# Gates and branch projections of two layers: from weights loaded and 256 token columns moving to tokens loaded and 512 weight columns moving

## What is computed

```python
h = rms_norm(x, norm1_g)
z = h @ w_in                      # the last 4 * 1024 columns of z are zg
...
ys = jnp.stack([ya, yb, yc, yd], axis=2)          # four branches, each 256 x 512
branches = jnp.einsum('bsnc,ncd->bsnd', ys, w_branch)   # four products of 512 x 1024
gates = jax.nn.sigmoid(zg.reshape(B, S, N_BRANCH_2, D_MODEL))
mix = jnp.sum(gates * branches, axis=2)
x = x + mix @ w_out
```

## Time and profile before

| | |
|---|---|
| median of 3 runs | 2144.68 us (2143.9 to 2147.41) |
| the profiled execution, its own time | 2145.49 us |
| its span, first to last instruction | 2144.2 us |
| TensorE (PE) busy | 2113.1 us, 99% |
| TensorE weight loads (PEld) busy | 1958.1 us, 91% |
| VectorE (DVE), ScalarE (ACT), GpSimd (POOL) busy | 65%, 58%, 46% |
| share of TensorE in the chain that ended last | 88% |
| mean granted TensorE clock | 0.998 |

### The profile page before, as it was taken

One profiled execution on the slowest core, in us unless ns is written; L12 is line 12 of the kernel. 1 busy time (PEld: TensorE's weight loads), 2 busy tenths in 40 slices (PEclk: granted clock), 3 DMA queues, 4 the chain that ended last, 5 costly groups with the idle time before them and its releaser, 6 DMA issues.

```text
span 2144.2 us, 37243 instructions
## 1 busy us (share of the span) xinstructions
PE 2113.1 (99%) x14292; PEld 1958.1 (91%) x14292; DVE 1395.7 (65%) x2706; ACT 1247.4 (58%) x2272; POOL 977.1 (46%) x791
## 2 busy tenths in 40 slices
PE   7999999999999999999999999999999999999999
PEld 7999989999999998888889899998888999998887
DVE  4467655998676756666667765557764864757874
ACT  5669454546777865455445465746555465756553
POOL 4776557999667650000004785660001876661000
PEclk9999999999999999999999999999999999999999
DMA  6444565655444456666665554555565645455565
GB/s 231 149 138 129 172 197 173 196 178 180 145 140 147 141 168 204 195 192 192 195 195 196 186 157 139 155 180 167 187 205 158 189 146 168 141 165 177 187 194 160
DMA packets 103952, 370.59 MB, mean 173 GB/s; under 512 B 11480, under 2 KB 12896, under 8 KB 103264
## 3 DMA queue, kind: packets, MB, share of 16 engines
q1 hardware_dynamic: 103776, 368.21, 54.8%
HBM read 366.05 MB, written 2.11 MB: 172 GB/s over the span
## 4 chain that ended last, share of the span: by engine, by line
PE 88%; DVE 6%; ACT 2%; POOL 1%; issue 1%; DMA 1%; SPq 0%; DVEq 0%; ACTq 0%; POOLq 0%
PE stream_bank L568 14%; PE stream_bank L570 14%; PE stream_bank L569 14%; PE side_bank L568 9%; PE side_bank L570 9%; PE side_bank L569 9%; PE side_bank L577 4%; PE stream_bank L577 4%; PE side_bank L574 2%; PE stream_bank L574 2%; PE side_bank L918 1%; PE side_bank L917 1%; POOL unit_lo L2606 1%; ACT unit_hi L1181 1%; PE side_bank L746 1%
## 5 line engine op out<-in xcount | busy, mean ns | idle before, releaser
L2606 POOL TENSOR_TENSOR unit_lo<-raw,unit_hi 128x512 fp32r<-128x512 f32 (+1 forms) x724 | 938.5, 1324 | 943.6 <-ACT unit_hi L1181 941.6
L1181 ACT ACTIVATE unit_hi<-raw 128x1024 fp32r<-128x1024 f32 (+1 forms) x678 | 708.9, 1046 | 199.5 <-PE side_bank L570 66.0
L1777 DVE TENSOR_TENSOR unit_lo<-raw,unit_hi 128x1024 fp32r<-128x1024 f32 (+1 forms) x316 | 390.3, 1236 | 227.9 <-ACT unit_hi L1181 225.9
L568 PE MATMUL stream_bank<-hT,unit_hi 128*128 128x256 f32 x1360 | 398.9, 293 | 1.8 <-POOL unit_lo L2606 1.8
L570 PE MATMUL stream_bank<-hT,unit_lo 128*128 128x256 f32 x1360 | 384.6, 283 | 0.0
L569 PE MATMUL stream_bank<-hT,unit_hi 128*128 128x256 f32 x1360 | 384.5, 283 | 0.0
L568 PE MATMUL stream_bank<-h2T,unit_hi 128*128 128x256 f32 x1024 | 293.3, 286 | 0.0
L570 PE MATMUL stream_bank<-h2T,unit_lo 128*128 128x256 f32 x1024 | 289.8, 283 | 0.0
L569 PE MATMUL stream_bank<-h2T,unit_hi 128*128 128x256 f32 x1024 | 289.6, 283 | 0.0
L568 PEld LDWEIGHTS stream_bank<-hT,unit_hi 128*128 128x128 f32 x1360 | 259.9, 191 | 3.6 <-POOL unit_lo L2606 2.0
L569 PEld LDWEIGHTS stream_bank<-hT,unit_hi 128*128 128x128 f32 x1360 | 260.0, 191 | 1.6
(11 more groups left out here) (392 smaller groups left out, 4303.9 us busy)
## 6 DMA issues: line engine op xcount, KB each, us to landing
raw<-in_peer_u_dram SPq DMA_DIRECT2D x128, 512.0 KB, 3.5
raw<-in_peer_v_dram SPq DMA_DIRECT2D x128, 512.0 KB, 4.1
raw<-in_gate_dram SPq DMA_DIRECT2D x64, 512.0 KB, 3.5
raw<-in_gt_dram SPq DMA_DIRECT2D x44, 512.0 KB, 3.5
raw<-in_up_dram SPq DMA_DIRECT2D x44, 512.0 KB, 3.5
raw<-in_ffn_out_dram SPq DMA_DIRECT2D x44, 512.0 KB, 3.5
raw<-in_branch_dram SPq DMA_DIRECT2D x32, 512.0 KB, 3.5
raw<-in_w_gate_dram SPq DMA_DIRECT2D x24, 512.0 KB, 3.5
```

Source lines behind the costliest of these rows:

```text
L568: mm(out, l.hi, r.hi, start=start, stop=False)
L1181: activation(k.unit_hi[n % SPLIT_SLOTS][:, 0:w], k.raw[n % RAW_SLOTS][:, 0:w], ACT.Copy).then_inc(k.sem("unit_hi"), 1)
L1777: V.tensor_tensor(k.unit_lo[s][:, 0:w], k.raw[n % RAW_SLOTS][:, 0:w], k.unit_hi[s][:, 0:w], ALU.subtract).then_inc(unit_lo, 1)
L2606: last = G.tensor_tensor(k.unit_lo[s][:, cols], k.raw[n % RAW_SLOTS][:, cols], k.unit_hi[s][:, cols], ALU.subtract)
```

## The change

1. The weight layouts of `gate` and `branch` become `tm_units(..., 2, 512)`. The number of units (32 + 16 in each layer) and their size stay.
2. A new `block_unit` multiplies them: 12 matmuls of 512 columns in place of 24 of 256. A block is 4 units of `gate` or 2 of a branch. It takes two of the three rotating banks, one for each token tile t; in each unit t = 0 comes first, so that the bank of t = 0 is finished half a unit before that of t = 1.
3. ScalarE evicts a whole block with two tanhs of 128 x 512 in the block's last round. In the other three rounds it does only `hi(n+3)` and its side steps.
4. VectorE sums a block in its last round (`add_branch`): for each of two banks a 128 x 512 product, and for branches 2 to 4 an addition.
5. The merged rows now have tokens on the partitions, and `w_out` needs features there: `turn_merged` turns them with 16 transposes of 128 x 128 in each layer, 8 behind the third unit of the last branch and 8 behind the first unit of `w_out`. ScalarE (`merged_hi`) and VectorE (`merged_lo`) split the turned banks.

The core of the diff:

```diff
+    def block_unit(key, block, units, u, lhs, banks):
+        i = block * units + u
+        n = U[key, i]
+        w = unit(n)
+        for t in range(TILES):
+            if u == 0:
+                banks.append(take(rotation[turn[0] % len(rotation)], (key, "block", block, t)))
+                turn[0] += 1
+            for c in range(2):
+                last = mm3(banks[t][:, :], lhs.at(lambda x: x[:, 2 * u + c, t * P:(t + 1) * P]),
+                           w.at(lambda x: x[:, c * 512:(c + 1) * 512]), u == 0 and c == 0, u == units - 1 and c == 1)
...
+    def turn_merged(label, x, half, ready):
+        for k2 in (2 * half, 2 * half + 1):
+            bank = take(SIDE + 2 + k2 % 2, (label, k2))
+            for t in range(TILES):
+                pe.wait_ge(*ready[2 * half + t])
+            for j in range(2):
+                c = 2 * k2 + j
+                for t in range(TILES):
+                    last = nc.tensor.transpose(bank[:, j * TOKENS + t * P:j * TOKENS + (t + 1) * P],
+                                               x[:, t, c * P:(c + 1) * P], k.ident)
+            last.then_inc(k.sem("merged_turned"), 1)
...
             for u in range(4):
                 tm_unit(key, half * 4 + u, lhs, 2 * u, 2, 512, banks, u == 0, u == 3, ready if half == 0 else None)
+                if half == 0 and u == 0 and behind_first is not None:
+                    behind_first()
...
# PE main()
-            for i in range(32):
-                fm_unit(name("gate"), i, k.hT2, KD)
-                yield
+            for block in range(8):
+                banks = []
+                for u in range(4):
+                    block_unit(name("gate"), block, 4, u, k.hT2, banks)
+                    yield
...
+                for half in range(2):
+                    banks = []
+                    for u in range(2):
+                        block_unit(name("branch"), 2 * n + half, 2, u, part, banks)
+                        if n == BRANCH_ORDER[-1] and half and u == 0:
+                            turn_merged(name("merged"), merged, 0, summed())
+                        yield
...
# ACT main()
-                evict(name("gate"), i, k.gates2[:, i, :], ACT.Tanh, scale=0.5)
+                advance(name("gate"), i)
+                if i % 4 == 3:
+                    for t in range(TILES):
+                        label = (name("gate"), "block", i // 4, t)
+                        act.wait_ge(*k.mm_done[label])
+                        activation(k.gates2[:, t, i // 4 * 512:(i // 4 + 1) * 512], k.bank[k.bank_of[label]][:, :], ACT.Tanh,
+                                   scale=0.5).then_inc(k.free[k.bank_of[label]], 1)
...
# DVE main(), and its add_branch
+                for i in range(KD // 2):
+                    advance(name("branch"), n * KD // 2 + i)
+                    if i % 2:
+                        add_branch(place, n, i // 2)
+                    if place == BRANCHES2 - 1 and i == 3:
+                        merged_lo(0)
+                    yield
...
+                dve.wait_ge(*k.mm_done[label])
+                if place == 0:
+                    V.scalar_tensor_tensor(gate, gate, 1.0, bank, ALU.add, ALU.mult).then_inc(k.free[b], 1)
+                    dve.wait_ge(*k.over[label])
+                else:
+                    own.then(V.scalar_tensor_tensor(bank, gate, 1.0, bank, ALU.add, ALU.mult))
+                    V.tensor_tensor(total, total, bank, ALU.add).then_inc(k.free[b], 1)
+                    dve.wait_ge(*k.over[label])
...
+        def merged_lo(half):
+            for k2 in (2 * half, 2 * half + 1):
+                b = SIDE + 2 + k2 % 2
+                dve.wait_ge(k.sem("mix_hi"), KD // 2 * l + k2 + 1)
+                V.scalar_tensor_tensor(k.hT2.lo[:, 2 * k2:2 * k2 + 2, :], k.bank[b][:, :].rearrange("p (a t) -> p a t", a=2),
+                                       0.5, k.hT2.hi[:, 2 * k2:2 * k2 + 2, :], ALU.mult, ALU.subtract).then_inc(k.free[b], 1)
```

More of the change, by code:

```diff
@@ L671, in close_banks @@
         at.unit = U[key, units - 1] + 1
+    def block_unit(key, block, units, u, lhs, banks):
[9 more added lines that the diff above has]
+                           w.at(lambda x: x[:, c * 512:(c + 1) * 512]), u == 0 and c == 0, u == units - 1 and c == 1)
+            if t == 0 and u == units - 1:
+                last.then_inc(tm_mm, 1)
+                tm_count[0] += 1
+                k.mm_done[key, "block", block, 0] = (tm_mm, tm_count[0])
+        last.then_inc(unit_mm, 1)
+        k.mm_done[key, "block", block, 1] = (unit_mm, n + 1)
+        at.unit = n + 1
+    def turn_merged(label, x, half, ready):
[9 more added lines that the diff above has]
+            last.then_inc(k.sem("merged_turned"), 1)
     def keep_warm(name):
@@ L1086, in swa @@
                 head(s, [(k.sem("swa_scaled"), 5 * l + 2 + s.column), k.over[name("sv"), 1]]) for s in heads])
+        merged = k.gates2[:, :, BRANCH_ORDER[0] * D:(BRANCH_ORDER[0] + 1) * D]
+        last_branch = lambda half, t: (name("branch"), "block", 2 * BRANCH_ORDER[-1] + half, t)
+        summed = lambda: {2 * h + t: k.over[last_branch(h, t)] for h in range(2) for t in range(TILES)
+                          if last_branch(h, t) in k.over}
         def main():
@@ L1698, in main @@
                     advance(name("branch"), n * KD // 2 + i)
[L1699 to L1702, removed]
+                    if n == BRANCH_ORDER[-1] and i == 3:
+                        merged_hi(0)
                     yield
@@ L1716, in sides, with merged_hi @@
             yield from at.finished(name("branch3"), swa())
+        def merged_hi(half):
+            for k2 in (2 * half, 2 * half + 1):
+                act.wait_ge(k.sem("merged_turned"), KD // 2 * l + k2 + 1)
+                split_hi(k.hT2.hi[:, 2 * k2:2 * k2 + 2, :],
+                         k.bank[SIDE + 2 + k2 % 2][:, :].rearrange("p (a t) -> p a t", a=2), "mix_hi", 0.5)
         at.run(main(), [bias_tables() if l == 0 else iter(()), own_channels(), sides()])
@@ L1720, in layer @@
             advance(name("w_out"), u)
+            if u == 0:
+                merged_hi(1)
         halves = [[((t, h), k.over[name("w_out"), h, t]) for t in range(TILES)] for h in range(2)]
@@ L2515, in main @@
                     yield
-                if place == 0:
[L2517 to L2536, removed]
@@ new lines, in main, with add_branch @@
+                for i in range(KD // 2):
[5 more added lines that the diff above has]
+                    yield
+        def add_branch(place, n, half):
+            for t in range(TILES):
+                label = (name("branch"), "block", 2 * n + half, t)
+                b = k.bank_of[label]
+                bank = k.bank[b][:, :]
+                gate = k.gates2[:, t, n * D + half * 512:n * D + (half + 1) * 512]
+                first = BRANCH_ORDER[0] * D + half * 512
+                total = k.gates2[:, t, first:first + 512]
+                if place == 0:
+                    dve.wait_ge(*k.over[name("gate"), "block", 2 * n + half, t])
+                dve.wait_ge(*k.mm_done[label])
[6 more added lines that the diff above has]
+                    dve.wait_ge(*k.over[label])
@@ L2552, in layer @@
         turned = norm_lo(name("n2"), name("norm2"), k.sumT)
-        add_out(name("w_out"), k.X, turned)
+        add_out(name("w_out"), k.X, turned, lambda: merged_lo(1))
         advance(name("w_out"), 7)
@@ L2935, in lay_out @@
         d[f"sq.{l}"], d[f"sk.{l}"], d[f"sv.{l}"] = fm_units(swa_q_columns(cut(7))), fm_units(cut(8)), tm_units(cut(9), 8, 128)
-        d[f"gate.{l}"] = fm_units(cut(10))
+        d[f"gate.{l}"] = tm_units(cut(10), 2, 512)
         b = wb[l].copy()
         b[3] = b[3].reshape(SWA_HEADS, SWA_DIM, D)[SWA_ORDER].reshape(MIX, D)
-        d[f"branch.{l}"] = np.concatenate([fm_unit_pairs(b[i]) for i in range(BRANCHES2)])
+        d[f"branch.{l}"] = np.concatenate([tm_units(b[i], 2, 512) for i in range(BRANCHES2)])
         d[f"w_out.{l}"] = tm_units(n["w_out_2"][l], 2, 512)
```

13 lines of the change are left out of this document (6 added, 7 removed).

## The result

The changed kernel takes 2147.11 us (median of 20 runs, 2145.34 to 2149.84), the kernel before, beside it, 2142.66 us (median of 20, 2139.11 to 2147.41). The ratio is 1.0019 with a 95% interval of 1.0013 to 1.0025. By the ratio that is +4.1 us (by the two medians +4.4) where +4.0 was forecast: a real loss, but one of only 0.2%.

The account below looks back on a forecast made before the run. TensorE, busy for 99% of the span, was taken as the bound. The terms -15.4 + 2.5 + 3.7 + 5.2 + 1.3 + 6.7 = +4.0 us made 2148.7 us from 2144.7, range 2139.5 to 2155.

Parts of the forecast that it names:

- The matmuls and their restarts: Gates and branches: wide matmuls save 15.4 us, 13.3 ns a merge; restarts behind side steps cost +2.5 us.
- The transposes: Four groups of eight for the merged rows, hidden by nothing: 0.92 us a group, +3.7 us.
- The turn ahead of `w_out`: TensorE waits for VectorE's `merged_lo` behind the last half's sum, until T + 2.6: +5.2 us in two layers.
- The gates' middle: Rounds 13 to 21: new 2.9 us wait in unit 20 for ScalarE's tanh, two old waits gone: +1.3 us.
- rival 2: Gates' middle: the new wait does not come, since ScalarE runs further ahead; 2139.5 us, chance 0.12.
- rival 3: Branches: VectorE holds the banks, sums slowed by contention with POOL; +4 to +12, 2153 to 2160 us, chance 0.15.
- The clock: Behind both new waits in each layer the clock falls: four times 1.7 us, +6.7 us, lower bound 0.
- rival 1: Both new waits come but the clock stays up: 2142.0 us (2145.3 if it falls only ahead of `w_out`); chance 0.25.
- The sum: Whole kernel, all terms together: +4.0 us, the median going from 2144.7 to 2148.7 us.

Follow-up runs that it names:

- e9: Changed kernel with each of its four groups of eight transposes issued twice: 2147.07 us, ratio 1.0024 to the kernel before.
- e1: Changed kernel with VectorE making `merged_lo(0)` ahead of the last block's last sum: 2138.55 us, ratio 0.9976 to the kernel before.
- e6: Changed kernel with the gates as before, so only the branches are changed: 2151.28 us, ratio 1.0037 to the kernel before.
- e8: Changed kernel with ScalarE's first tanh ahead of the high part in round 15 alone: 2143.25 us, ratio 0.9992 to the kernel before.
- e2: Changed kernel with ScalarE's first tanh ahead of the high part in every block's last round: 2139.64 us, ratio 0.9983 to the kernel before.
- e4: Changed kernel with ten unused wide matmuls filling TensorE's wait ahead of `w_out`: 2142.52 us, ratio 0.9995 to the kernel before.
- e5: Kernel before with only the gates changed to blocks of wide matmuls: 2138.64 us, ratio 0.998 to the kernel before.
- e7: Changed kernel with ScalarE's first tanh ahead of the high part in round 19 alone: 2141.4 us, ratio 0.9991 to the kernel before.
- e12: Changed kernel with `merged_lo(0)` ahead of the last sum and the tanh first in round 19 alone: 2134.4 us, ratio 0.9957 to the kernel before.
- e10: Changed kernel with `merged_lo(0)` ahead of the last sum and tanh first in every block's last round, second run, another chip: 2129.16 us, ratio 0.9937.

## Why the prediction was right

- **The matmuls and their restarts.** Right. From the first gate unit to the end of unit 12 (1266.74 to 1308.03) TensorE takes 41.28 us in place of 43.01: -1.73, where 13 x 0.16 less the restarts makes 1.8. Three gate units on end take 8.16 us, 2.72 each. The Trainium skill ("TensorE: Matmul & The Clock Gate", section "Back-to-back issue gap") gives the fixed part of 2.5 ns for an isolated gap and says that in a stream of weight loads and matmuls both set the spacing; the prediction read it as the stream's. This stream shows 13.3 ns.
- **The transposes.** 0.79 us to the next matmul, with the slower restart behind them 0.9 a group; forecast 0.92. e9 gives 0.11 for one more.
- **The turn ahead of `w_out`.** Right in all its steps. Let T be the last matmul's start and 0.23: 1426.08. The product of t = 0 began at T - 1.11 (forecast T - 1.09), the first low part ended half-way through its 1.29, at T + 2.4 (T + 2.53), and TensorE went on at T + 2.63 (T + 2.6). e1 and e6 confirm size and cause.
- **The gates' middle.** The square root began at 1310.66, the reciprocal 3.08 us behind the end of unit 12 (forecast 3.07). From it to the tanh of block 4 it is 1332.77 - 1311.11 = 21.66 us (21.69). The wait is 2.56 us of idle (2.7), since a tanh of 128 x 512 ends 0.54 to 0.6 behind its start and not 0.65. From the end of unit 12 to the first matmul behind unit 21 (1340.52) it is 32.5 us with the clock's part; 31.2 + 1.7 = 32.9 was forecast. Against the prediction, rival 2 was treated too lightly: "the chain is VectorE's, which gains nothing" holds for this kernel, but e8 shows 1.8 us of that chain to be GpSimd's doing. Those rows stood in the profile before as well (the same product at 1.41, 1.50 and 1.51 us, and 0.42 where GpSimd was idle). For rival 3 I looked at the contention, and only at operations with an operand in PSUM, which don't suffer it. That the 21.69 us held was luck in this respect: in e8 a shift of the high part by 1.8 us makes the chain 1.8 us shorter and the kernel, by the ratios, 5.8 us faster than the changed one.
- **The clock.** The size of one fall was right to a tenth: 1.7 us in every fall but one. The sum of 6.7 was right for this kernel, as both its profiles show all four falls. The reason was wrong. The prediction took an idle of 1.89 us or more as enough and one of 1.76 as harmless. In the profiles of the other kernels the clock fell behind only 7 of 18 idles of the same 2.46 to 2.56 us (e1 1 of 2, e2 1 of 2, e4 0 of 2, e5 1 of 2, e6 2 of 2, e7 0 of 2, e8 1 of 2, e9 1 of 4). Idles of 1.7 to 2.1 us that the change doesn't touch show the same, in both directions (last section). So rival 1, with its chance of 0.25, was not far off: it is what e4 and e7 show at all their idles of this length. That the term came out at 6.7 is in part luck. The eight falls of eight in this kernel's two profiles are not eight separate trials either, as the four restarts lie the same distances apart in both, within 0.2 us.
- **The sum.** By layer 0: -1.73 to unit 12 (forecast -1.8), +0.68 in the middle (+1.08), +0.32 to `w_out` (+0.13), +2.59 in `w_out` (+2.62): +1.86 against +2.03; two layers and the end +3.9 against +4.0. The largest error is the 0.4 us of the middle, and it cancels in part. The time itself, 2147.1 in place of 2148.7, is off because the three runs shown of before had a median of 2144.7, 2 us above that of the 20 runs of which they are the first.

## What to carry to other kernels

When matmuls are merged into larger blocks, the saving is a fixed part for each, read from the distances of starts; the price is that banks are finished and freed in pairs, so look in every consumer's program for what stands ahead of the first bank's release, and put that release first. Here two such reorderings turned a loss of 4 us into a gain of 14. An idle of TensorE of 2.5 us cost here from 2.5 to 4.2 us, once 5.9, so it wants a range and not one price; and contention has to be read for the very operands on the chain, in the rows of before.

## What the runs showed of the hardware

**VectorE beside GpSimd.** A product of two 128 x 256 operands in SBUF took 0.41 to 0.43 us alone and 1.40 to 1.52 when it began beside GpSimd's low part of 1.27 a piece; products and sums of 128 x 512 with an operand in PSUM took their 0.69 to 0.70 either way. The Trainium skill, "SBUF — State Buffer", section "SBUF: two separate sides", says that the port pair the two engines share is locked for a whole instruction, and that a VectorE operation with two inputs in SBUF needs it against a GpSimd operation that reads SBUF. The traces agree: what is added (0.97 us) is within one piece of GpSimd's work, and in e8, where the product begins 0.03 us ahead of GpSimd, it is GpSimd's low part that takes longer, 2.79 in place of 2.54 us.

**The clock behind an idle.** Windows of e7 behind idles of 1.62 and 2.46 us:

```profile
1332.00:1334.00 2.00, 1.65 (x7) 1.40 (x8) 1.93 (x6) 1.98 (x4) 0.68 (x1) 1.00 0.57 172
1334.00:1336.00 2.00, 2.00 (x11) 1.65 (x10) 1.27 (x4) 1.99 (x6) 2.00 (x2) 1.00 0.23 94
1426.00:1428.00 2.00, 1.89 (x8) 1.61 (x9) 1.70 (x2) 0.00 (x0) 0.00 (x0) 1.00 0.26 104
1428.00:1430.00 2.00, 2.00 (x14) 1.74 (x13) 0.00 (x0) 0.41 (x1) 0.00 (x0) 1.00 0.63 201
```

It stayed at 2.4 GHz behind all four idles of 1.61 to 1.62 us (e7, e12) and both of 0.77 (e8) in the layers, and fell to 1.2 GHz behind 15 of 26 of 2.46 to 2.56, 8 of 8 in the changed kernel. A fall cost 1.7 us each time, but once 3.4, in e1:

```profile
1332.00:1334.00 2.00, 1.02 (x3) 0.83 (x3) 1.89 (x7) 1.98 (x4) 1.48 (x2) 0.58 0.66 219
1334.00:1336.00 2.00, 2.00 (x6) 1.62 (x5) 1.71 (x3) 1.63 (x6) 1.03 (x1) 0.50 0.12 47
1336.00:1338.00 2.00, 2.00 (x6) 1.52 (x6) 1.60 (x7) 2.00 (x5) 0.72 (x1) 0.50 0.80 262
1338.00:1340.00 2.00, 2.00 (x8) 1.58 (x7) 0.92 (x2) 2.00 (x8) 2.00 (x2) 0.71 0.00 0
```

The length of the idle is not what decides, and no length from 1.74 us on was safe. Ahead of the layers, in code that no version changes, all 14 profiles have the same three idles. Behind the one of 2.05 to 2.09 us the clock fell in 4 (before, e4, e8, e10), behind the one of 1.89 in 9, and behind the one of 1.58 to 1.76 in 2 (e8, e9). The changed kernel behind 2.05 us, and then e9 behind 1.75, timeline and window of each:

```profile
787.58 0.47 PE L568 MATMUL side_bank<-unit_hi,expert_pair 128*128 128x512 f32 x1 [2.05 <-DVE experts L2299]
788.00:792.00 4.00, 4.00 (x20) 3.28 (x19) 2.11 (x4) 2.29 (x3) 0.00 (x0) 1.00 0.61 218
...
67.95 0.49 PE L568 MATMUL stream_bank<-hT,unit_hi 128*128 128x256 f32 x1 [1.75 <-POOL unit_lo L2680]
68.00:70.00 2.00, 2.00 (x10) 2.00 (x11) 1.90 (x5) 0.00 (x0) 1.43 (x7) 0.52 0.52 117
```

What decides at the same length of idle stays open.
